# Turning the normalized tokens: VectorE scales them in place and TensorE transposes, instead of fp32 products with a diagonal matrix

## What is computed

```python
h = jnp.concatenate([meta, x], axis=1)              # (1, 528, 2048)
def rms_norm(x, w):
    xf = x.astype(jnp.float32)
    y = xf * lax.rsqrt(jnp.mean(xf * xf, axis=-1, keepdims=True) + RMS_EPS)
    return (y * w.astype(jnp.float32)).astype(x.dtype)
proj = rms_norm(h, norm_mix_w) @ w_in               # 2048 -> 9232 columns
```

## Time and profile before

| what | value |
|---|---|
| runs (3) | 2696.96, 2700.0 and 2703.47 us, median 2700.0 us |
| span of the profiled execution | 2699.0 us |
| TensorE busy | 2646.7 us (98% of the span) |
| VectorE busy | 1835.7 us (68%) |
| ScalarE busy | 1007.2 us (37%) |
| GpSimd busy | 344.1 us (13%) |
| chain that ended last | TensorE 91%, VectorE 2%, issue 2%, DMA 2% |

### The profile page before, as it was taken

One profiled execution on the slowest core, in us unless ns is written; L12 is line 12 of the kernel. 1 busy time (PEld: TensorE's weight loads), 2 busy tenths in 40 slices (PEclk: granted clock), 3 DMA queues, 4 the chain that ended last, 5 costly groups with the idle time before them and its releaser, 6 DMA issues.

```text
span 2699.0 us, 44506 instructions
## 1 busy us (share of the span) xinstructions
PE 2646.7 (98%) x17640; PEld 2419.6 (90%) x17640; DVE 1835.7 (68%) x1775; ACT 1007.2 (37%) x1045; POOL 344.1 (13%) x350
## 2 busy tenths in 40 slices
PE   8999999999999999999998999999999999999998
PEld 7999988888888987878888999999999998788886
DVE  4444545555554233548889888888888888888898
ACT  4443322222222232223354444444444444333334
POOL 5000044444442420101000000000000000000000
PEclk9999999999999999999999999999999999999999
DMA  4333222222223433679524445444544459866562
GB/s 138 102 88 91 79 79 79 82 81 78 78 78 86 109 94 117 221 268 319 187 103 133 150 161 171 155 152 148 179 148 155 151 172 305 292 205 203 175 196 104
DMA packets 345656, 398.75 MB, mean 148 GB/s; under 512 B 11481, under 2 KB 300386, under 8 KB 344418
## 3 DMA queue, kind: packets, MB, share of 16 engines
q1 hardware_dynamic: 285970, 333.30, 39.3%
q10 hardware_dynamic: 59616, 64.49, 7.0%
HBM read 325.92 MB, written 71.83 MB: 147 GB/s over the span
## 4 chain that ended last, share of the span: by engine, by line
PE 91%; DVE 2%; issue 2%; DMA 2%; ACT 1%; SPq 1%; POOL 1%; DVEq 0%; ACTq 0%; POOLq 0%
PE psum L2082 33%; PE psum L2399 10%; PE psum L2401 10%; PE psum L2400 10%; PE psum L2374 6%; PE psum L2375 6%; PE psum L2376 6%; PE psum L2242 2%; PE psum L2237 1%; DMA w_raw<-in_w_proj_a 1%; PE psum L2031 1%; PE psum L2059 1%; DMA dn_raw<-in_w_ffn_down 1%; PE psum L2221 1%; PE psum L2314 1%
## 5 line engine op out<-in xcount | busy, mean ns | idle before, releaser
L2082 PE MATMUL psum<-hn_hi,w_hi 128*128 128x264 f32 (+1 forms) x1600 | 450.7, 330 | 0.0
L2082 PE MATMUL psum<-hn_lo,w_hi 128*128 128x264 f32 (+1 forms) x1600 | 449.9, 330 | 0.0
L2082 PE MATMUL psum<-hn_hi,w_lo 128*128 128x264 f32 (+1 forms) x1600 | 449.9, 330 | 0.0
L1347 DVE TENSOR_TENSOR w_lo<-w_raw,w_hi 128x1024 fp32r<-128x1024 f32 x144 | 186.6, 1297 | 253.5 <-ACT w_hi L901 253.0
L901 ACT ACTIVATE w_hi<-w_raw 128x1024 fp32r<-128x1024 f32 x144 | 152.1, 1057 | 373.7 <-PE psum L2082 345.5
L2082 PEld LDWEIGHTS psum<-hn_lo,w_hi 128*128 128x128 f32 x1600 | 269.1, 188 | 22.7 <-issue 0.7
L2082 PEld LDWEIGHTS psum<-hn_hi,w_lo 128*128 128x128 f32 x1600 | 268.9, 188 | 22.4
L2082 PEld LDWEIGHTS psum<-hn_hi,w_hi 128*128 128x128 f32 x1600 | 269.1, 188 | 22.0 <-issue 0.2
L2374 PE MATMUL psum<-dn_hi,act_hl 128*128 128x512 f32 x616 | 240.2, 390 | 4.3 <-DVE hq L1684 2.5
L2376 PE MATMUL psum<-dn_hi,act_hl 128*128 128x512 f32 x616 | 239.8, 389 | 0.0
L2375 PE MATMUL psum<-dn_lo,act_hl 128*128 128x512 f32 x616 | 239.8, 389 | 0.0
(11 more groups left out here) (355 smaller groups left out, 6400.5 us busy)
## 6 DMA issues: line engine op xcount, KB each, us to landing
w_raw<-in_w_in SPq DMA_DIRECT2D x144, 512.0 KB, 3.9
ffn_raw<-in_w_ffn_gate SPq DMA_DIRECT2D x44, 1024.0 KB, 6.5
ffn_raw<-in_w_ffn_up SPq DMA_DIRECT2D x44, 1024.0 KB, 6.7
dn_raw<-in_w_ffn_down SPq DMA_DIRECT2D x32, 1024.0 KB, 8.3
act_hl<-act_dram SPq DMA_DIRECT2D x56, 512.0 KB, 9.0
act_dram<-comb_hi ACTq DMA_DIRECT2D x22, 896.0 KB, 4.2
act_dram<-comb_lo ACTq DMA_DIRECT2D x22, 896.0 KB, 6.2
out_raw<-in_w_out SPq DMA_DIRECT2D x16, 1024.0 KB, 9.8
```

The source lines that it names most:

```text
L1347: dve.tensor_tensor(wlo[s][:], raw[s][:], whi[s][:].bitcast(F32), ALU.subtract).then_inc(S["lo_ready"], 1)
L2082: ins = pe.matmul(o, lhs, r, start=kt == 0 and i == 0, stop=kt == 4 * n_chunks - 1 and i == 2)
```

## The change

VectorE multiplies a whole token tile by `rms[u]` in place (`scale_rows`, one instruction of up to 128x2048 where a 128x128 one wrote the diagonal), and TensorE turns the scaled tile with `transpose` against the identity. Both stand at the same places of their engines' orders as the instructions that they replace, with the same semaphores. The number of instructions in the program is the same on both engines; in the trace one fp32 product of before leaves two records. The second norm keeps its diagonals and its products. The five diagonals of the first norm are no longer placed in memory.

```diff
-            def diagonal(u, rows=P):
-
+            def diagonal(t):
+
+                u = TT + 1 + t
                 dve.wait_ge(S["x_rms"], u + 1)
-                dve.tensor_scalar(diag[u][0:rows, 0:rows], ident[0:rows, 0:rows], rms[0:rows, u:u + 1], None,
-                                  ALU.mult).then_inc(S["x_diag"], 1)
+                dve.tensor_scalar(diag[t][:, :], ident[:, :], rms[:, u:u + 1], None, ALU.mult).then_inc(S["x_diag"], 1)
...
+            def scale_rows(u, rows=P):
+
+                dve.wait_ge(S["x_rms"], u + 1)
+                dve.tensor_scalar(xt[u][0:rows, :], xt[u][0:rows, :], rms[0:rows, u:u + 1], None, ALU.mult) \
+                    .then_inc(S["x_diag"], 1)
+
             for m in range(2):
                 dve.memset(conv_in[m][:, 0:CONV - 1], 0.0).then_inc(S["vectors_more"], 1)
-            diagonal(0, META)
-            diagonal(1)
+            scale_rows(0, META)
+            scale_rows(1)
             dve.wait_ge(S["vectors_ready"], 2)
             for u in range(TT + 1):
                 if 2 <= u + 1 <= TT:
-                    diagonal(u + 1)
+                    scale_rows(u + 1)
                 weight_quads(u, xy, nmix, x_tokens(u), META if u == 0 else P)
...
                     for i in range(4):
                         k = 4 * q + i
-                        ins = pe.matmul(turn_bank(u, q)[:, i, 0:rows], src(k)[0:rows, :],
-                                        diag[u][0:rows, 0:rows], start=True, stop=True)
+                        out = turn_bank(u, q)[:, i, 0:rows]
+                        if u <= TT:
+                            ins = pe.transpose(out, src(k)[0:rows, :], ident[0:rows, 0:rows])
+                        else:
+                            ins = pe.matmul(out, src(k), diag[u - TT - 1][:, :], start=True, stop=True)
                     ins.then_inc(S["x_turned"], 1)
```

More of the change, by code:

```diff
@@ L230, in hybrid_block @@
         xy = [place(f"xy{i}", [P, 4, P], at=tmp_at + i * 2048) for i in range(4)]
-        diag = [place(f"diag{i}", [P, P], at=ext_at + 4608 + 512 * i) for i in range(TT + 1)]
-        diag += [place(f"diag{TT + 1 + i}", [P, P], at=(mixer_consts_at + 8704 if i < 2 else hn_at + 64 + 5 * 16384) + 512 * i)
-                 for i in range(TT)]
+        diag = [place(f"diag{i}", [P, P], at=(mixer_consts_at + 8704 if i < 2 else hn_at + 64 + 5 * 16384) + 512 * i)
+                for i in range(TT)]
         assert mixer_consts_at + 8704 + 1024 <= hn_at
@@ L1823, in _ @@
                 sum_of_h(t)
-                diagonal(TT + 1 + t)
+                diagonal(t)
             t_two(0, 0)
```

## The result

The changed kernel takes 2710.3 us (median of 12 runs, 2702.2 to 2716.0), the one before 2700.3 us (12 runs). The ratio is 1.0038, with a 95% interval of 1.0028 to 1.0047: 10 us slower. The prediction had 2697.4 us, a range of 2693 to 2702 and 0.04 for slower. It was wrong.

What follows compares the result with a forecast made beforehand. TensorE was taken to bound the kernel, with only its start moving: -3.6 us for tile 2's earlier `xy` and +1.0 for one more scale gave -2.6, so 2696.4 us, plus 1.0 for the median: 2697.4 us, range 2693.0 to 2702.0.

Steps and rivals of the forecast that it cites:

- the moment 42.67 us: TensorE's return for good behind the start, forecast to move to about 40.1 us, all later work only shifting.
- a change of over 5 us: Sign on the kernel's total time: a change this large would mean that something outside the start moved.
- Scales of 128x2048 at 1.3 us: VectorE's in-place scale of a token tile takes 1.3 us, adding 1.0 to 1.1 us over the instruction replaced.
- rival 1: VectorE's scales run at the two-operand pace, 2.3 us each: +0.9 us, 2700.9 us; chance 0.10.
- The second scale costs nothing: At the start, `scale_rows(1)` runs 10.2 to 11.5 us in VectorE's idle time ahead of 12.12 us.
- `xy` of tile 2 at 20.1: On VectorE at the start, it begins at 20.1 us where it began at 23.69: 3.6 us earlier.
- Transposes cost half: TensorE's turning of token tiles takes 0.24 us each at the lower clock, where a product took 0.43.
- rival 2: Transposes save nothing on TensorE, which bounds until 21.5 us; scales add 2.0 us, later start 0.2: 2702.2 us; chance 0.04.
- rival 3: TensorE's clock stays low since transposes do not raise it: -0.3 to +1.4 us, 2700.5 in the middle; chance 0.25.
- rival 4: TensorE's low clock stretch at 43 us goes, worth 1.7 us: change worth -4.3 us, 2695.7 us; chance 0.11.
- A rule against a row: VectorE and GpSimd slow each other; `scale_rows(3)` meeting GpSimd's `hn_lo` takes 0.3 us longer, sum -2.3 instead of -2.6.
- The stated resolution: A measurement of the whole kernel can tell about 0.2% (5.4 us) from no change; three runs spread over 6.5 us.

Runs made afterwards that it cites:

- e3: The kernel before with 49 small 16x16 transposes added at TensorE's start, 98 instructions more: 2712.45 us, ratio 1.0047.
- e1: The changed kernel with every transpose of the first norm issued twice into the same place: 2697.05 us, ratio 0.9986.
- e7: The changed kernel with 32 small 16x16 transposes, 64 instructions, added at TensorE's start: 2693.2 us, one run.
- e2: The changed kernel with 40 small 16x16 transposes, 80 instructions, added at TensorE's start: 2696.21 us, ratio 0.9984.
- e6: The changed kernel with 16 small 16x16 transposes, 32 instructions, added at TensorE's start: 2717.8 us, one run.
- e4: Half of the change: VectorE scales in place, TensorE turns by fp32 products with the plain identity instead of transposes: 2702.0 us, ratio 1.0004.
- e5: The changed kernel with 40 small transposes behind the delta-rule loop, ahead of the merge: 2705.65 us, ratio 1.0029.
- e9: The changed kernel with 40 small transposes at TensorE's start, and tiles 3 and 4 scaled by ScalarE instead of VectorE: 2695.09 us, ratio 0.9979.

## Why the prediction was wrong

**The step that failed** is in its first part: "After 42.67 us TensorE has its work lined up and only follows. So the whole question is: by how much does the moment 42.67 us move? All else is a shift of the rest." The rest did not only shift. The change also took 160 instructions out of TensorE's program ahead of the loop, and so moved the loop by 160 instructions against the borders of the blocks in which instructions are fetched. That cost 12.9 us in the profiled run, five times what the start gave. The text ahead of the prediction has the error at its root: it says that the number of instructions in the program is the same on both engines and takes the second record of an fp32 product for a matter of the trace. For VectorE that is so (x1775 in both pages); for TensorE the second record is a second instruction, and leaving it out moved the loop. None of the rivals had it, and my sentence that a change of over 5 us would mean that something outside the start moved is all that was right about it.

It could have been foreseen as a risk. The kernel before shows 770 weight loads and 771 products in one pass of the loop:

```profile
500.00:631.40 131.40, 131.40 (x771) 114.57 (x770) 69.75 (x112) 34.02 (x53) 55.50 (x48) 1.00 0.28 80
```

With registers, branches and waits one pass has 1604 instructions, six blocks of 256 and 68 over; this is my count of the program, which no profile shows. The instruction packets are 16 KB each (48 are 0.79 MB). The Trainium skill, Runtime: NRT & Kernel Launch, Instruction fetch mechanics, states that instructions come in blocks of 16 KiB (256 of them), that TensorE holds 128 KiB, that the next block is fetched while the current one runs, and that a taken branch to a block outside the current window of two forces a fetch before the engine goes on. The size of the packets agrees, and so do the pauses at the loop's edge. The window of two does not: the loop of the kernel before is over six blocks long and branches back between 475 and 606 us without one packet. An estimate from that page's 128 KiB is that eight blocks are held, so that a loop that touches seven fits with the block fetched ahead, and one that touches eight does not (nine). The nine packets in each pass fit this estimate; the runs do not show the capacity itself.

What the runs do show is where the loop stands well. Call its place in the kernel before 0 and count on by the edits (two instructions a transpose), modulo 256 (the changed kernel and e3 are 258 apart by the edits, and behave alike). Places 0 (before, e1), 160 (e7) and 176 (e2) ran well; 96 (changed), 98 (e3) and 128 (e6) did not. The bad stretch is at least 33 places long, then, and at most 159; the 67 that was expected with e6 lies between, and is not shown.

**Point by point:**

- *Scales of 128x2048 at 1.3 us*: 1.27 to 1.29 us. Right; rival 1 (2.3 us) is out.
- *The second scale costs nothing, `scale_rows(3)` starts at 18.9 and `xy` of tile 2 at 20.1*: 19.42 and 20.61. The `hn_lo` pair of tile 1 took 2.38 us beside GpSimd's and not 1.47, 0.9 us that I had not put in, while tile 0 was done 0.3 us sooner. The same contention was smaller at tile 2 (2.38 instead of 2.80), which gave 0.4 back: errors of both signs, and a sum that was right by some luck, 40.09 for 40.1.
- *Transposes cost half*: they did; rival 2 is out. The timeline of TensorE, the answer to the earlier trace rows:

```profile
9.05 1.88 PE L2038 MATMUL psum<-ident,xt 16*128 16x16 f32 x16 [0.28 <-DVE xt L1371]
12.47 5.58 PE L2038 MATMUL psum<-ident,xt 128*128 128x128 f32 x32 [1.54 <-DVE xy L1359]
21.44 2.36 PE L2038 MATMUL psum<-ident,xt 128*128 128x128 f32 x16 [3.39 <-DVE xy L1359]
26.85 0.56 PE L2067 MATMUL psum<-hn_hi,w_hi 128*128 128x264 f32 x1 [3.05 <-DVE w_lo L1346]
```

  Tile 0 with its 16 rows took 0.12 us each even at the lower level, not 0.24; that was worth nothing: the `xy` of tile 0 waited for ScalarE's copy of the weights until 12.10 us, as before (12.12).
- *The clock* (rival 3): transposes did bring it up. Their records in the changed kernel that start in 12 to 14 us, and in 21 to 24 us:

```profile
L2038 PE MATMUL psum<-ident,xt x8: 421/421/445, 12.5 to 14.0; 128*128 128x128 f32 x8
```

```profile
L2038 PE MATMUL psum<-ident,xt x16: 272/273/329, 21.4 to 23.5; 128*128 128x128 f32 x16
```

  421 ns, then 272, with nothing but transposes on the engine between; the records change from one to the other near 16 us, without a pause ahead. What the Trainium skill states there (TensorE: Matmul & The Clock Gate, PE-mode transpose) does not hold for these fp32 transposes. After the pause of 3.05 us ahead of 26.85 the clock was low again, for the first 3 us of chunk 0 (0.50 from 26.8 to 29.9), and VectorE hid it; the pause of 3.39 us ahead of 21.44 had brought no such stretch.
- *The low stretch at 43 us* (rival 4): it stayed in the profiled run of the changed kernel, where the 48 products from 40.09 on take 7.60 us. In e4, e5, e7 and e9 it is gone (6.07 or 6.08 us for 48), so it comes and goes as rival 4 had it, worth some 1.5 us.
- *A rule against a row*: the slowing of VectorE and GpSimd beside each other is real, but it fell on `hn_lo`. No scale met GpSimd's `hn_lo` of a whole tile: `scale_rows(3)` started at 19.42, and the `hn_lo` of tile 1 had ended at 18.95. So 1.27 us does not show what a scale costs beside it, and the 0.3 us left in the range for that stay untested.
- *The stated resolution*: single runs scatter by 3 to 8 us to either side of their median, but the difference of the medians, 10 us, is clear of that by its interval (1.0028 to 1.0047). The range was drawn around the start alone.

## What to carry to other kernels

When an edit changes how many instructions an engine has ahead of a long loop, compare the instruction queue's packets before and after; if they rise, look for "issue" pauses at the loop's edges before judging the edit by its time. A few harmless instructions in idle time ahead of the loop tell the cost of the edit from that of the loop's new place, and here they turned a loss of 0.4% into a gain of 0.16%.

## What was not expected of the hardware

- Thirty-two instructions in idle time were worth 25 us (e6 against e7), one run each.
- A pause of 2.6 us cost 4.3, since the lower clock followed it; one of e5's pauses brought no lower clock and cost less.
- Small fp32 transposes are cheap: 40 of 16x16 are done in 1.23 us at the kernel's start (e2):

```profile
1.59 1.23 PE L2105 MATMUL psum<-ident 16*16 16x16 f32 x40 [1.59 <-POOL ident L709]
```

- The time from TensorE's return to the landmark takes values of 973 to 977 us among the runs without the pauses, without any difference in the work. The profiles differ there in the clock. The kernel before around 340 us and around 43 us:

```profile
330.00:350.00 20.00, 16.68 (x91) 14.67 (x91) 14.64 (x28) 7.30 (x12) 7.55 (x6) 0.83 0.15 41
38.00:48.00 10.00, 7.40 (x48) 7.18 (x48) 6.07 (x7) 3.75 (x6) 9.07 (x16) 0.83 0.52 152
```

  and e7, with no lower clock, though TensorE's pauses ahead were no shorter (3.37 and 2.93 us, where they were 3.32 and 2.60 before):

```profile
330.00:350.00 20.00, 16.63 (x102) 14.40 (x101) 15.06 (x29) 7.89 (x15) 9.85 (x8) 1.00 0.20 53
38.00:48.00 10.00, 7.85 (x64) 7.64 (x65) 3.66 (x4) 1.25 (x2) 8.55 (x23) 1.00 0.37 107
```

  What decides whether the clock falls is open; it was not tried. It is a share of what single runs scatter by. Of the 25 us of e6 against e7 some 1.6 are this (7.63 us for the 48 products from 40.14 on in e6, 6.08 in e7); around 340 us both run at 1.00.
